# A hybrid decoder trunk on one core: inversion levels in shared tiling trips, the old state added by an identity product, and the RWKV side tiles in another order

## The reference

```python
def step(state, inp):                    # RWKV-7, one token; the kernel takes chunks of 64 tokens
    r_t, w_t, k_t, v_t, kk_t, kka_t = inp
    s_kk = jnp.einsum('bhvk,bhk->bhv', state, kk_t)
    state = state * w_t[:, :, None, :] - s_kk[..., None] * kka_t[:, :, None, :] + v_t[..., None] * k_t[:, :, None, :]
    return state, jnp.einsum('bhvk,bhk->bhv', state, r_t)

sol = lax.linalg.triangular_solve(lower, rhs, left_side=True, lower=True, unit_diagonal=True)   # GDN, each chunk
```

## Time and profile before

| | us |
|---|---|
| median of three runs | 3284.78 |
| lowest, highest | 3279.73, 3286.07 |
| the profiled execution | 3283.6 |
| its span, first to last instruction | 3281.8 |
| PE busy, PE weight loads busy | 3181.3, 2796.3 |
| DVE, ACT, POOL busy | 2291.9, 1716.0, 253.7 |
| mean granted TensorE clock, share of full speed | 0.996 |

### The profile page before, as it was taken

The page is one execution under the profiler, slowest core; times in us unless marked ns, Lnnn a source line. Parts: engine busy times, 40 slices in busy tenths (PEclk is TensorE's granted clock), DMA queues, the critical chain, the costliest instruction groups (busy, mean ns, idle before and its releaser), DMA issues. The chain is left out here.

```text
span 3281.8 us, 74221 instructions
## 1 busy us (share of the span) xinstructions
PE 3181.3 (97%) x24946; PEld 2796.3 (85%) x24946; DVE 2291.9 (70%) x5014; ACT 1716.0 (52%) x3645; POOL 253.7 (8%) x246
## 2 busy tenths in 40 slices
PE   8999999999999999999999999999999999999998
PEld 7888888889897888888788888888898978888886
DVE  5777676666886677777667776766668766777776
ACT  5555454432395555555556554544324955555554
POOL 2211111110000000000022211111100000000000
PEclk9999999999999999999999999999999999999999
DMA  3232323224224555555432232322242255555553
GB/s 132 99 105 85 106 91 102 76 93 167 84 76 154 186 192 187 185 190 192 153 116 90 99 105 86 109 91 91 70 173 90 71 176 187 189 191 191 186 187 127
DMA packets 122237, 433.35 MB, mean 132 GB/s; under 512 B 15744, under 2 KB 18048, under 8 KB 121344
## 3 DMA queue, kind: packets, MB, share of 16 engines
q1 hardware_dynamic: 122112, 431.74, 37.8%
HBM read 430.64 MB, written 1.05 MB: 132 GB/s over the span
## 5 line engine op out<-in xcount | busy, mean ns | idle before, releaser
L2404 PE MATMUL bank<-x_both,u_parts 128*128 128x512 f32 x1536 | 557.9, 397 | 1.8 <-DVE u_parts L2524 1.8
L2388 PE MATMUL bank<-v_parts,act_high 128*128 128x512 f32 x1024 | 405.7, 396 | 4.0 <-DVE v_parts L2529 2.6
L2390 PE MATMUL bank<-v_parts,act_low 128*128 128x512 f32 x1024 | 399.9, 391 | 0.0
L2400 PE MATMUL bank<-x_both,u_parts 128*128 128x256 f32 x1536 | 399.6, 281 | 0.0
L2524 DVE TENSOR_TENSOR u_parts<-u_raw,u_parts 128x512 fp32r<-128x512 f32 x384 | 265.6, 692 | 191.2 <-ACT u_parts L2459 191.0
L2389 PE MATMUL bank<-v_parts,act_high 128*128 128x512 f32 x1024 | 398.9, 390 | 0.0
L335 PE MATMUL bank<-x_parts,w_parts 128*128 128x256 f32 x1248 | 394.7, 316 | 1.1 <-DVE w_parts L320 1.1
L336 PE MATMUL bank<-x_parts,w_parts 128*128 128x256 f32 x1248 | 352.2, 282 | 0.0
L337 PE MATMUL bank<-x_parts,w_parts 128*128 128x256 f32 x1248 | 351.7, 282 | 0.0
L2529 DVE TENSOR_TENSOR v_parts<-v_raw,v_parts 128x512 fp32r<-128x512 f32 x512 | 330.1, 686 | 30.7 <-ACT v_parts L2466 27.4
L2404 PEld LDWEIGHTS bank<-x_both,u_parts 128*128 128x128 f32 x1536 | 288.5, 188 | 62.6 <-issue 2.6
(11 more groups left out here) (376 smaller groups left out, 6293.4 us busy)
## 6 DMA issues: line engine op xcount, KB each, us to landing
v_raw<-in_v SPq DMA_DIRECT2D x256, 512.0 KB, 3.5
u_raw<-in_u SPq DMA_DIRECT2D x192, 512.0 KB, 4.2
ring<-in_w_side SPq DMA_DIRECT2D x80, 512.0 KB, 3.5
ring<-in_w_gdn SPq DMA_DIRECT2D x64, 512.0 KB, 3.5
ring<-in_w_rwkv SPq DMA_DIRECT2D x48, 512.0 KB, 5.9
ring<-in_w_gdn_side SPq DMA_DIRECT2D x32, 512.0 KB, 3.5
ring<-in_u SPq DMA_DIRECT2D x32, 512.0 KB, 3.7
u_ring<-in_u SPq DMA_DIRECT2D x32, 512.0 KB, 3.5
```

The costliest lines, as they stand in the source:

```text
L2388: te.matmul(ps, f32r(w_hi), f32r(x_hi), start=start, stop=False, **kw)
L2390: return te.matmul(ps, f32r(w_lo), f32r(x_hi), start=False, stop=stop, **kw)
L2400: return te.matmul(banks[r % 4][:, T:2 * T], f32r(u_lo[:, cols]), f32r(xhigh[:, k]), start=False, stop=stop)
L2404: mm = te.matmul(banks[r % 4][:, :].rearrange("p (x t) -> p x t", x=2), f32r(u_hi[:, cols]), f32r(x_both[:, :, k]), start=(k == 0), stop=( ...
```

## The change

`invert64_pe` makes X of level lev + 1 directly behind Y and YT of level lev, in one stretch of 64x64 tiling, and both fills of a level stand behind its X. In RWKV the first X stands directly behind AV, with the bonus product and the two fills of AV behind it. A further product `ident @ St` (chunks 1 and 2) adds the old state in the accumulator, and one DVE operation scales and masks in place of three. The side tiles are now f1 before T0, f0 and f2 in the chunk steps, f3 and f4 (POOL's) after them, and six k-steps of f4 behind the transposition of the outputs. Low and high parts move with them: f1 of the next block at the end of a body, f0 in the inversion, f2 in chunk steps 2 and 3. SP loads r, k, v two bodies ahead.

```diff
-        for lev in range(1, N_LEVELS):
-            t = f"inv{lev}"
-            te.wait_ge(G.sem, G.at(f"{t}mask", i))
+        def product(lev):
+            te.wait_ge(G.sem, G.at(f"inv{lev}mask", i))
             te.wait_ge(*((S.sem, S.at("invT", i)) if lev == 1 else (V.sem, V.at(f"inv{lev - 1}T", i))))
             te.sem_inc(passed, 1)
-            blocks(bX, NLM[:, lev - 1], T_).then_inc(E.sem, E.one(f"{t}X"))
+            blocks(bX, NLM[:, lev - 1], T_).then_inc(E.sem, E.one(f"inv{lev}X"))
+
+        product(1)
+        for lev in range(1, N_LEVELS):
             fill(lev, 0)
-            te.wait_ge(S.sem, S.at(f"{t}X", i))
+            fill(lev, 1)
+            te.wait_ge(S.sem, S.at(f"inv{lev}X", i))
             if lev > 1:
                 te.wait_ge(V.sem, V.at(f"inv{lev - 1}TT", i))
             te.sem_inc(passed, 1)
             if whole or lev < N_LEVELS - 1:
-                blocks(bY, TT, X).then_inc(E.sem, E.one(f"{t}Y"))
-            blocks(bYT, X, TT).then_inc(E.sem, E.one(f"{t}YT"))
-            fill(lev, 1)
+                blocks(bY, TT, X).then_inc(E.sem, E.one(f"inv{lev}Y"))
+            blocks(bYT, X, TT).then_inc(E.sem, E.one(f"inv{lev}YT"))
+            if lev < N_LEVELS - 1:
+                product(lev + 1)
 
...
+    SIDES = ("f3", "f4", "f1", "f0", "f2")
...
-        number = {"r": 0, "k": 1, "v": 2, "f2": 9, "f3": 10, "f4": 11}
+        number = {"r": 0, "k": 1, "v": 2, "f1": 5, "f0": 9, "f2": 10}
...
+                def next_tiles(i):
                     for s, what in enumerate("rkv"):
                         W.free(sp, tile(what, i - 1))
                         rwkv_tile(sp, l, i, s)
...
+                def other_tiles(i, ahead):
                     sp.wait_ge(E.sem, E.before("gate", i))
                     sp.dma_start(small, A["rwkv_up"][l, i]).then_inc(loaded[3], 16)
...
+                    if ahead:
+                        next_tiles(i + 1)
+                    for what in ("f0", "f2"):
+                        W.free(sp, tile(what, i - 1))
+                        rwkv_side_tile(sp, l, i, SIDES.index(what))
+                    if ahead:
+                        first_side(i + 1)
+                    for n in range(2):
+                        sp.wait_ge(EF.sem, EF.before(SIDES[n], i))
...
+                next_tiles(1)
+                first_side(1)
+                with sp.Fori(1, NI - 1) as i:
+                    other_tiles(i, True)
+                other_tiles(NI - 1, False)
...
-                    if more and (lev, y) == (5, 0):
+                    if more and (lev, y) == (5, 1):
                         pe_sums(te, i + 1)
...
-                side(0, 1)
...
-                side(*range(2, 16))
+                side("f1", *range(KT))
...
-                te.matmul(b7[:, 0:T], blk64, rk, start=True, stop=True).then_inc(E.sem, E.one("bonus"))
-                fill(0, 0)
-                fill(0, 1)
-                invert64_pe(te, E, S, V, G, i, NLM, T_, TT, X, b2, b3, b4, fill)
-                te.wait_ge(V.sem, V.at("inv5TT", i))
-                te.wait_ge(S.sem, S.at("AVO", i))
-                te.sem_inc(passed, 1)
+
+                def first_fill(lev, y):
+                    if (lev, y) == (1, 0):
+                        te.matmul(b7[:, 0:T], blk64, rk, start=True, stop=True).then_inc(E.sem, E.one("bonus"))
+                        fill(0, 0)
+                        fill(0, 1)
+                    fill(lev, y)
+
+                invert64_pe(te, E, S, V, G, i, NLM, T_, TT, X, b2, b3, b4, first_fill)
...
-                left = list(range(16, 40))
-                step_side = lambda n: side(*(left.pop(0) for _ in range(n)))
+                left = [(what, k) for what in ("f0", "f2") for k in range(KT)]
+
+                def step_side(n):
+                    for _ in range(n):
+                        side(*left.pop(0))
+
+                step_side(2)
+                te.wait_ge(V.sem, V.at("inv5TT", i))
+                te.wait_ge(S.sem, S.at("AVO", i))
+                te.sem_inc(passed, 1)
...
                         te.matmul(b5[:, 0:P], KR[:, b, 0], St, start=True, stop=True).then_inc(E.sem, E.one(f"R{q}"))
+                        step_side(1)
                         if q > 1:
                             te.wait_ge(V.sem, V.at(f"o{q - 2}", i))
                         te.matmul(OB[hf][:, 0:P], KR[:, b, 1], St, start=True, stop=False, skip_group_check=True)
-                        step_side(1)
                         te.wait_ge(V.sem, V.at(f"R{q}", i))
                         te.sem_inc(passed, 1)
...
                     if q < 3:
                         te.matmul(b2[:, 0:P], BK[:, 2 + b], VX[:, hf, b], start=True, stop=False)
-                    step_side(1)
+                        if q:
+                            te.matmul(b2[:, 0:P], ident, St, start=False, stop=False)
+                    step_side((1, 0, 0, 2)[q])
                     te.wait_ge(S.sem, S.at(f"U{q}", i))
...
-                side(*left)
+                step_side(len(left))
+                side("f3", *range(KT))
+                side("f4", 0, 1)
...
-                if not more:
-                    turn(te, b2, 5)
+                side("f4", *range(2, KT))
...
                     if more and n == 1:
+                        act_round(a, i + 1, "k")
                         act_gates(a, i + 1)
-                        act_side_round(a, i + 1, 0)
+                    if n == 1:
+                        act_side_round(a, i, 0)
                     if more and n in (2, 4):
...
-                        act_side_round(a, i + 1, 1)
+                    if n == 2:
+                        act_side_round(a, i, 1)
...
                             W.skip(a, W.high, tile("r", NI), 3)
-                        act_round(a, i, "f2")
+                        act_round(a, i, "f0")
...
-                if more:
-                    act_round(a, i + 1, "r")
...
-                    act_round(a, i + 1, "k")
-                act_side(a, i, 0)
+                    act_round(a, i + 1, "r")
+                act_side(a, i, 1)
...
+                        act_round(a, i, "f2")
+                act_side(a, i, 0)
                 a.activation(no_root, ones[:, 0:1], ACT.Sqrt).then_inc(S.sem, S.one())
+                if more:
+                    act_round(a, i + 1, "f1")
...
-                act_side(a, i, 3)
+                act_side(a, i, 2)
...
                 def fill(n):
-                    if more and n == 2:
+                    if more and n == 1:
                         vec_decays(v, i + 1)
-                        vec_piece(v, i + 1, 0)
+                    if n == 2:
+                        if more:
+                            vec_piece(v, i + 1, 0)
+                            vec_rest(v, i + 1, "v")
+                        else:
+                            W.skip(v, W.low, tile("r", NI), 3)
                     if more and n == 3:
-                        vec_rest(v, i + 1, "v")
                         vec_factors(v, i + 1)
                     if more and n == 4:
                         vec_piece(v, i + 1, 1)
                         vec_squares(v, i + 1)
+                    if n == 4:
+                        vec_rest(v, i, "f0", (0,))
+                    if more and n == 4:
                         vec_sums(v, i + 1)
-                    if n == 2 and not more:
-                        W.skip(v, W.low, tile("r", NI), 3)
                     if n == 5:
-                        vec_rest(v, i, "f2")
-                    if more and n == 5:
-                        vec_roots(v, i + 1, 0)
-
-                tt = lambda o, a0, a1, op, label=None: v.tensor_tensor(o, a0, a1, op).then_inc(V.sem, V.one(label))
+                        vec_rest(v, i, "f0", (1,))
+
...
-                if more:
-                    vec_rest(v, i + 1, "r", (0,))
...
-                    vec_rest(v, i + 1, "r", (1,))
-                    vec_rest(v, i + 1, "k")
+                    vec_rest(v, i + 1, "r")
+                vec_taps(v, i)
                 v.wait_ge(E.sem, E.at("bonus", i))
                 v.tensor_tensor(bv, b7[:, 0:T], Z[:, 2], ALU.mult).then_inc(V.sem, V.one("bv"))
-                vec_taps(v, i)
+                if more:
+                    vec_rest(v, i + 1, "k")
...
                         if q == 1 and more:
                             vec_piece(v, i + 1, 2)
-                            vec_bonus(v, i + 1)
-                        if q == 2:
-                            vec_rest(v, i, "f3")
+                            vec_roots(v, i + 1, 0)
                         if q == 2 and more:
                             vec_roots(v, i + 1, 1)
+                        if q > 1:
+                            vec_rest(v, i, "f2", (q - 2,))
                         if q == 3 and more:
                             vec_key(v, i + 1)
-                            vec_beta(v, i + 1)
-                        out_add(q - 1)
-                        if q == 3:
```

(31 more changed lines are left out.)

92 lines of the change are left out of this document (37 added, 55 removed).

## The result

The changed kernel takes 3305.38 us (median of four, 3301.48 to 3307.26) where the kernel before, measured beside it, takes 3283.65 (3279.73 to 3286.07): ratio 1.0066, 95% interval 1.0048 to 1.0083. A second set later gave 3303.73 against 3281.05, ratio 1.0080 (1.0066 to 1.0094). The change makes the kernel slower by 22 us, and the forecast was 3305. How far the way to that number was the forecast one is the matter of what follows.

What follows compares the result with a forecast made beforehand. The prediction took PE, busy for 97% of the span, its own list and its few waits as the bound. GDN +14 and RWKV +7 (+3.5 a layer) made +21 us on 3283.6, stated as 3305, range 3280 to 3324.

Steps and rivals of the forecast that it cites:

- GDN, +14: GDN inversion levels: the moved fill uncovers a wait for the next tile's low half, +2.3 us in each of six loop blocks.
- The wait for f2's low half, +2.0: RWKV chunk 2: PE waits behind R for the half DVE makes late, +2.0 us a loop block, +1.1 in the two last.
- Removed waits, -1.85: RWKV chunk steps: waits before chunk 3, chunks 1 and 2 and the transposition go, -1.85 us a block.
- the identity products, +0.4: RWKV chunks 1 and 2: the two added `ident @ St` products take 0.2 us each, +0.4 a block.
- The 0.15 for k-step 4 in chunk 3: RWKV chunk 3: k-step 4 waits for half 1 of f2, some 0.15 us.
- The levels in RWKV, -0.2 - 0.05 + 0.3: RWKV inversion, us a block: first X's saved trip -0.2, joined levels -0.05, T's addition late from v's low part beside POOL +0.3.
- The last block, +0.6: Last RWKV block of each layer: +1.1 us for the f2 wait, the rest saved, +0.6 in all.
- Start and tail, -1.4 and -0.9 a layer: RWKV layer: before the first block -1.4 us, POOL no longer beside DVE; k-steps behind the last transposition -0.9.
- The rival of the clock, +1.7 in each of 14 blocks: RWKV loop blocks: PE's idle lowers the clock, about +1.7 us each, 3329; clock or a further wait, above 3320: 0.10.
- f2 does not hold: Rival, RWKV chunk 2: f2's half is ready, no wait, time 3276; chance 0.13 shared with trips paying.
- trips pay in full: Rival, RWKV and GDN inversions: no wait for T or a low half, about 3250; chance 0.13 shared with f2 not holding.

Runs made afterwards that it cites:

- ident_alone: The kernel before with only the identity product adding the old state in RWKV's chunk steps 1 and 2 and one DVE operation for up to three: ratio 0.9972.
- two opposite experiments: GDN's joined trips undone in the changed kernel, ratio 1.0028; GDN's joined trips alone put into the kernel before, ratio 1.0045.
- f2_half_early: The changed kernel with DVE making f2's low half 0 in chunk step 1 and the reciprocal's halves moved to steps 2 and 3: ratio 0.9962.
- gdn_joined_alone: The kernel before with the joined trips in GDN and nothing else of the change: ratio 1.0045.
- rwkv_old_levels: The changed kernel with RWKV's inversion levels in separate trips again, first X still behind AV, GDN still joined: ratio 1.0071.
- both_low_first: The changed kernel with f2's low half 0 made in chunk step 1 and GDN's low parts made ahead of each level's additions: 3257.74 us, ratio 0.9923.

## Why the prediction was right, and where only its sum was

**GDN, +14: right in mechanism, place and size.** A level was to take 5.34 and takes 5.34. A loop block was to grow by 2.3 and grows by 2.27, six times, 13.6 us. The parts fit too: the trip was to take 1.86 with X's wait in it and takes 1.91, and the k-steps then start 2.27 behind Y as said (555.06 to 557.33). From the last Y to the tile behind level 5 it is 2.84, as said (576.40 to 579.24). What the prediction left out is the last block of GDN, which has no next tile to wait for: from its first products to its transposition it takes 39.17 where it took 39.72 in layer 2, 0.55 less.

**The wait for f2's low half, +2.0: right, 1.94.** The half is ready 2.17 behind R, said to be 2.35. The reciprocal runs ahead of it, as the prediction had it.

**Removed waits, -1.85, and the identity products, +0.4: the removed waits were under-counted.** Both waits went, and the product costs 0.23 against 0.2. But all RWKV edits apart from the f2 wait bring -1.66 a block, where the terms of the prediction make -1.25. The row at the transposition accounts for 0.35 of the difference: before, the product behind it started 0.50 us later, now a k-step starts 0.14 later. The prediction counted the wait before the transposition and took the six k-steps of f4 behind it as neutral; that they also fill the gap behind it was missed. The 0.15 for k-step 4 in chunk 3 did not come either, the joining of the levels came 0.06 cheaper than said (below), and the two products and the first X some 0.06 dearer each: together about the 0.41 between the two sums. That the gap was filled by those k-steps is read from the rows; no run isolates it.

**The levels in RWKV, -0.2 - 0.05 + 0.3: the joining right in size, its cause in part wrong.** For the joining of the levels with the low half beside POOL +0.25 was said, and +0.19 measured. The -0.2 for the first X no run isolates; by PE's rows it is -0.14 (from AV to the first Y 5.23 us before, 5.81 now with two k-steps more, 0.72). The delay passed on to X is not that of v's low half: the addition to T behind it is not late, and the level that it lies in takes 3.52. It is the decays' operation of 1.33 us, ahead of the addition one level earlier. So it is an operation drawn out beside POOL, as said, but another one (1.33 us beside POOL, 0.42 without). This cause is read from the rows, and no run moves that operation.

**The last block, +0.6: failed.** It is +1.71. The f2 wait is 1.30 there (1.1 said), but "the rest saved" was taken over from the loop blocks: the last block has no waits to remove, and ident_alone shows it 0.42 longer.

**Start and tail, -1.4 and -0.9 a layer: right in sum, and one in the wrong place.** The first transposition comes 1.94 earlier (91.29 to 89.35). A fall from 43.95 to 47.36 lies in that stretch, the equal of some 1.7 us, so the list itself is 3.6 shorter there. That includes the first block, 0.28 longer, so the stretch ahead of it is some 3.9 shorter. The tail is 1.24 longer: in layer 2, where neither kernel has a fall, 50.50 us lay between the last transposition and GDN's first block, and now 51.74. The six k-steps leave the first block and come back behind the last transposition. Together that is -2.6 against -2.3.

**The rival of the clock, +1.7 in each of 14 blocks: partly true.** The prediction gave a clock or a further wait 0.10 and its forecast nothing. It costs 1.5 a fall, in three to eight blocks a run. Undisturbed, RWKV costs (-3.6 with the first block, + 6 x 0.28 + 1.71 + 1.24) = +1.0 a layer, where +3.5 was said, so +2 and not +7 for two. Three falls in loop blocks (+4.5), the one at 43.95 (+1.7) and the late DMA (+1.9) then bring RWKV to some +10 in this profile. Against that the kernel before had two falls outside the RWKV blocks (at 419.7 and 658.6) that after has not, -3.4. The last GDN blocks take 1.1 us less (two of 0.55), and 1.8 us less lie behind the last transposition of GDN in layer 2, where the change touches nothing. With GDN's 13.6 that is 17.4 of the 17.9 by which the span grew.

So of the 22 us, 14 were forecast rightly and shown by two opposite experiments. The other 8 were forecast at 7 from the lists alone, and are about 2 from the lists, 4 to 9 from a lowered clock (three to six falls of 1.5), which the wait on f2 brings about, and 2 to 3 from the falls ahead of the first blocks, less the 6 us that the kernel before had and after has not (3.4, 1.1 and 1.8 above). That the sum still met 3305 is luck in this part: over-counted terms stood in for a clock that the forecast had left out. The rivals "f2 does not hold" and "trips pay in full" are refuted by the 1.78 us in the rows and by f2_half_early, gdn_joined_alone and rwkv_old_levels. The price of the second, about 3250, comes out only with the wait on f2 kept, which its own condition excludes.

## What to carry to other kernels

When work is moved past a wait, list for each moved piece what it was hiding and what its own operand waits for: both losses here, 2.27 us in GDN and 1.94 in RWKV, were a half tile that DVE made too late, and each was cured by moving one line of DVE's list. Before joining two trips, look whether the second trip reads what another engine makes of the first: if so, the saved switches come back as a wait: joining cost 0.19 us a block in RWKV, and in GDN, with the wait for the low half cured, a joined level took 4.96 us against 4.94. A last, peeled iteration has to be costed by its own waits, and a standing time that recurs in a loop by more than its length.

## What the runs showed of the hardware that was not expected

- Idle time of 1.78 us in the middle of dense work brought the granted clock down to 0.50 behind it in 29 of 70 blocks. The 2.55 us idle ahead of the first block left it at 1.00 in the kernel before, but the same 2.55 us in ident_alone had a fall behind it, and so had the 2.56 us in gdn_joined_alone (at 42.70): a fall came behind two of the six such waits (2.4 to 2.6 us) of the three kernels that have them. So one stretch that kept its clock says little. Filling the same time with unread products removed the falls from the loop blocks without delaying the chain there. Busy time by stretch in ident_alone, the wait and the fall:

```profile
35.95:38.50 2.55, 0.00 (x1) 0.03 (x1) 2.52 (x4) 0.87 (x1) 1.67 (x2) 1.00 0.00 0
39.68:43.09 3.41, 3.11 (x15) 2.84 (x14) 1.99 (x4) 1.93 (x3) 0.00 (x0) 0.50 0.42 154
```

- A fall in an RWKV loop block costs 1.5 us. In the one shown (221.44 to 224.85) the same kinds of products take up to twice the time: a k-step's matmuls follow each other at 0.21 us (223.76 to 223.97) where they follow at 0.12 in other blocks.
- The 1.35 and 0.54 us for a DMA of small weights occurred in two blocks of after, and 1.6 in one of both_low_first. The kernel before shows none. SP's order was changed by the change; whether that is the cause was not tried, and it stays open.
